# A decoder trunk on one core: the opening with x normalised ahead of its transposition, modulation tiles of two chunks, and every eighth tile summed on TensorE

## The reference

```python
h = rms_norm(x, g_pre) * (1.0 + scale) + shift
y = rms_norm(fn(h), g_post)
x = x + res_w * gate * y
```

## Time and profile before

| | us |
|---|---|
| median of three runs (lowest, highest) | 1993.89 (1992.87, 1994.47) |
| the profiled execution | 1992.25 |
| its span, first to last instruction | 1990.5 |
| PE busy in the span | 1892.8 (95%) |
| DVE busy | 1403.8 (71%) |
| ACT busy | 845.7 (42%) |

### The profile page before, as it was taken

One profiled execution on the slowest core, in us unless ns is written; L12 is line 12 of the kernel. 1 busy time (PEld: TensorE's weight loads), 2 busy tenths in 40 slices (PEclk: granted clock), 3 DMA queues, 4 the chain that ended last, 5 costly groups with the idle time before them and its releaser, 6 DMA issues.

```text
span 1990.5 us, 21378 instructions
## 1 busy us (share of the span) xinstructions
PE 1892.8 (95%) x8554; PEld 1538.5 (77%) x8554; DVE 1403.8 (71%) x1469; ACT 845.7 (42%) x1075; POOL 22.6 (1%) x29
## 2 busy tenths in 40 slices
PE   2679999999999999999999999999999999999997
PEld 2558878878878878777777787788888888888895
DVE  4997888878878878765766566666666665555556
ACT  2214434444443443474565533743444434443443
POOL 0000000000000000000000000000000000000000
PEclk7879999999999999999999999999999999999999
DMA  9898998998989988645333444566666665555551
GB/s 343 308 332 324 352 342 319 360 339 328 340 332 346 338 342 325 217 138 181 127 111 127 161 136 170 185 236 233 247 240 233 236 208 190 190 190 190 196 196 74
DMA packets 204131, 486.83 MB, mean 245 GB/s; under 512 B 8049, under 2 KB 21121, under 8 KB 188929
## 3 DMA queue, kind: packets, MB, share of 16 engines
q1 hardware_dynamic: 202816, 482.79, 68.0%
q10 hardware_dynamic: 992, 2.63, 0.4%
q0 software_dynamic: 224, 0.06, 0.0%
HBM read 483.31 MB, written 2.10 MB: 244 GB/s over the span
## 4 chain that ended last, share of the span: by engine, by line
PE 87%; DVE 5%; DMA 3%; issue 2%; ACT 1%; DVEq 0%; SPq 0%; POOLq 0%; POOL 0%; ACTq 0%
PE ps_g L1381 10%; PE ps_u L1381 10%; PE ps_u L1383 9%; PE ps_u L1382 9%; PE ps_g L1383 9%; PE ps_g L1382 9%; PE ps_t L1381 4%; PE ps_t L1382 4%; PE ps_t L1383 4%; PE ps_y L1383 4%; PE ps_y L1381 4%; PE ps_y L1382 4%; DVE arena L1144 2%; DMA ada_raw<-in_ada_w 2%; DVE w_lo L857 1%
## 5 line engine op out<-in xcount | busy, mean ns | idle before, releaser
L857 DVE TENSOR_TENSOR w_lo<-w_raw,w_hi 128x1024 fp32r<-128x1024 f32 (+1 forms) x632 | 752.9, 1200 | 481.0 <-ACT w_hi L509 479.8
L509 ACT ACTIVATE w_hi<-w_raw 128x1024 fp32r<-128x1024 f32 (+1 forms) x632 | 657.4, 1042 | 945.5 <-PE ps_u L1383 335.8
L1381 PE MATMUL ps_g<-w_hi,xT_hi 128*128 128x512 f32 (+1 forms) x880 | 346.9, 394 | 21.2 <-DVE w_lo L857 11.1
L1381 PE MATMUL ps_u<-w_hi,xT_hi 128*128 128x512 f32 (+2 forms) x880 | 348.1, 396 | 16.7 <-DVE w_lo L857 15.9
L1383 PE MATMUL ps_u<-w_hi,xT_lo 128*128 128x512 f32 (+2 forms) x880 | 342.3, 389 | 0.0
L1382 PE MATMUL ps_u<-w_lo,xT_hi 128*128 128x512 f32 (+2 forms) x880 | 341.8, 388 | 0.0
L1383 PE MATMUL ps_g<-w_hi,xT_lo 128*128 128x512 f32 (+1 forms) x880 | 340.8, 387 | 0.0
L1382 PE MATMUL ps_g<-w_lo,xT_hi 128*128 128x512 f32 (+1 forms) x880 | 340.5, 387 | 0.0
L881 DVE SCALAR_TENSOR_TENSOR arena<-ada_raw,cond,arena 128x2048 f32<-128x2048 f32 x108 | 253.5, 2347 | 24.4 <-DMA ada_raw<-in_ada_w 24.2
L1381 PEld LDWEIGHTS ps_g<-w_hi,xT_hi 128*128 128x128 f32 x880 | 165.9, 189 | 64.8 <-DVE w_lo L857 18.6
L1381 PEld LDWEIGHTS ps_u<-w_hi,xT_hi 128*128 128x128 f32 x880 | 167.0, 190 | 55.7 <-DVE w_lo L857 19.6
(11 more groups left out here) (242 smaller groups left out, 1542.3 us busy)
## 6 DMA issues: line engine op xcount, KB each, us to landing
w_raw<-in_ffn_w_in SPq DMA_DIRECT2D x160, 1024.0 KB, 5.1
ada_raw<-in_ada_w SPq DMA_DIRECT2D x128, 1024.0 KB, 7.3
w_raw<-in_ffn_w_out SPq DMA_DIRECT2D x80, 1024.0 KB, 5.1
w_raw<-in_mix_w_in SPq DMA_DIRECT2D x32, 1024.0 KB, 5.1
arena<-in_ada_w SPq DMA_DIRECT2D x16, 1024.0 KB, 10.2
w_raw<-in_mix_w_out SPq DMA_DIRECT2D x16, 1024.0 KB, 5.0
w_raw<-in_ffn_w_in SPq DMA_DIRECT2D x16, 768.0 KB, 4.5
w_raw<-in_ffn_w_out SPq DMA_DIRECT2D x8, 768.0 KB, 4.4
```

The costliest lines, as they stand in the source:

```text
L509: nc.scalar.activation(w_hi[:, u % 4, 0:n, 0:width], w_raw[:, s, 2 * hf:2 * hf + n, 0:width], ACT.Copy).then_inc(hi_done, 1)
L857: nc.vector.tensor_tensor(w_lo[:, u % 4, 0:n, 0:width], w_raw[:, s, 2 * hf:2 * hf + n, 0:width], w_hi[:, u % 4, 0:n, 0:width].bitcast(F32) ...
L1381: nc.tensor.matmul(o, a_hi[:, k, rows], w_hi[:, b, c, 0:width], start=start, stop=False)
```

## The change

- ACT's queue loads x in two halves instead of one piece; the four constant loads move to SP, after the tenth hidden block of the first SwiGLU, and DVE's wait for them to the token mixer.
- c has its own small load, transposition and semaphore, so that `cond` is made ahead of the other small columns.
- ACT squares x first. DVE makes the variance, POOL the power, ACT writes x times its row norm (128 x 2048, twice) into `yacc`, and only then PE transposes, into all eight PSUM banks. ACT copies the eight banks after the last transposition. The diagonal, its matmuls, `rbc` and `xt_scale` are gone.
- An `ada_w` tile now is two chunks of both vectors (two loads of 512 KB). DVE adds a chunk of both vectors in one operation of 128 x 1024, 14 operations a strip instead of 32, each waiting for the one before. The eighth tile of a strip isn't added on DVE: PE multiplies it by `cond` in the sums, 24 matmuls a strip instead of 16.
- A slot that the eighth tile used is loaded again only after the sums.
- After the columns, ACT makes scale and shift in one operation (two of 128 x 256, in place), waits for it, and copies 128 x 512 into `xT_hi`; DVE subtracts in one operation of 128 x 512.

```diff
-PRE_USES = 8
+PRE_USES = 16
-ADA_PRE = 32
+STRIP_TILES = 8
+STRIP_SUMMED = 7
+ADA_PRE = STRIPS * STRIP_SUMMED
@@ SP, a strip
-                for a in range(8):
-                    kg, m = divmod(a, 2)
-                    count = 8 * s + a
-                    need(sp, ada_done, count - 3)
-                    sp.dma_start(first_slots[a % 4]..., four chunks of one vector).then_inc(ada_landed[a % 4], 16)
+                for i in range(STRIP_TILES):
+                    if i % 4 == 3 and (s or i == 7):
+                        if i == 3:
+                            sp.wait_ge(cols_done, s)
+                        else:
+                            sp.wait_ge(ada_done, STRIP_SUMMED * s + 4)
+                    elif i >= 4:
+                        sp.wait_ge(ada_done, STRIP_SUMMED * s + i - 3)
+                    elif s:
+                        sp.wait_ge(ada_done, STRIP_SUMMED * (s - 1) + i + 5)
+                    for m in range(2):
+                        slot = first_slots[i % 4][:, m * 2 * NB:(m + 1) * 2 * NB].rearrange("p (k n) -> p k n", k=2)
+                        sp.dma_start(slot, ...[:, 2 * i:2 * i + 2, m * D + s * NB:m * D + (s + 1) * NB]).then_inc(ada_landed[i % 4], 16)
@@ ACT
+            def first_xt_hi(b):
+                act.wait_ge(modcol_done, b // 2 + 1)
+                for c in range(2):
+                    k = 2 * b + c
+                    ins = nc.scalar.activation(xT_raw[:, k, :], xT_raw[:, k, :], ACT.Identity, bias=modcol[:, 0, 1, k:k + 1],
+                                               scale=modcol[:, 0, 0, k:k + 1])
+                link(ins)
+                nc.scalar.activation(xT_hi[:, 2 * b:2 * b + 2, :], xT_raw[:, 2 * b:2 * b + 2, :], ACT.Copy).then_inc(xt_hi_done, 1)
...
+            first_x_squares()
+            act.wait_ge(rstd_ready, 1)
+            for t in range(TILES):
+                nc.scalar.activation(yacc[:, t, :], x_sb[:, t, :], ACT.Copy, scale=rstd[:, 2 + t:3 + t]).then_inc(xn_first, 1)
+            act.wait_ge(xt_done, 8)
             for b in range(8):
...
@@ DVE
+            def first_ada(s, i):
                 before = chain[0]
+                for k in range(2):
                     if k == 0:
+                        dve.wait_ge(ada_landed[i % 4], 32 * (2 * s + i // 4) + 32)
+                        need(dve, ada_done, STRIP_SUMMED * s + i if i else 0)
                     else:
+                        dve.wait_ge(dve_chain, before + 1)
+                    part = acc[:, 1:3, s * NB:(s + 1) * NB]
+                    raw = first_slots[i % 4].rearrange("p (m k n) -> p m k n", m=2, k=2)[:, :, k, :]
+                    weight = cond[:, 2 * i + k:2 * i + k + 1]
...
@@ PE, the sums of a strip
+                pe.wait_ge(ada_landed[3], 32 * (2 * s + 2))
+                pe.wait_ge(ada_done, STRIP_SUMMED * (s + 1))
                 for m in range(2):
+                    for c in range(4):
+                        for kk in range(2):
+                            nc.tensor.matmul(col, last[:, m, kk, c * P:(c + 1) * P], cond[:, 2 * STRIP_SUMMED + kk:2 * STRIP_SUMMED + kk + 1],
+                                             start=kk == 0, stop=False)
+                        ins = nc.tensor.matmul(col, acc[:, MODS_PRE[m][1], k * P:(k + 1) * P], ones[:, 0:1], start=False, stop=True)
```

More of the change, by code:

```diff
@@ L122, in build @@
         kvg = sb("kvg", [P, KV_RANK])
[L123 removed]
+        small_rows = sb("small_rows", [7 * KD, P])
         more_rows = sb("more_rows", [2 * KD, P])
@@ L1110, in xt_lo @@
-            def xt_lo(n, b):
-                def f():
-                    dve.wait_ge(xt_hi_done, 8 * n + b + 1)
-                    dve.wait_ge(xt_scaled, 8 * n + b + 1)
-                    for c in range(2):
-                        k = 2 * b + c
-                        last = nc.vector.scalar_tensor_tensor(xT_lo[:, k, :], junk[:, (k % 8) * SEQ:(k % 8 + 1) * SEQ], modcol[:, n, 1, k:k + 1],
-                                                              xT_hi[:, k, :].bitcast(F32), ALU.add, ALU.subtract)
-                    last.then_inc(xt_lo_done, 1)
-                return f
@@ L1121, in _ @@
-            dve.wait_ge(cond_ready, 1)
-            dve.wait_ge(const_landed, 16 * 4)
-            dve.wait_ge(ident_landed, 16)
-            nc.vector.tensor_scalar(negsink[:, :], sink[:, :], -1.0, None, ALU.mult)
-            def first_ada(s, kg):
+            def first_ada(s, i):
                 before = chain[0]
-                for i in range(8):
-                    k, m = divmod(i, 2)
-                    count = 8 * s + 2 * kg + m
-                    slot = (2 * kg + m) % 4
+                for k in range(2):
@@ L1133, in first_ada @@
                     if k == 0:
-                        dve.wait_ge(ada_landed[slot], 16 * (count // 4) + 16)
-                        if kg:
-                            dve.wait_ge(ada_done, count - 1)
-                    else:
-                        dve.wait_ge(dve_chain, before + i - 1)
-                    part = acc[:, MODS_PRE[m][1], s * NB:(s + 1) * NB]
-                    raw, weight = first_slots[slot][:, k * NB:(k + 1) * NB], cond[:, 4 * kg + k:4 * kg + k + 1]
-                    if kg == 0 and k == 0:
+                        dve.wait_ge(ada_landed[i % 4], 32 * (2 * s + i // 4) + 32)
@@ L1464, in gate_rows @@
                 ins.then_inc(gbc_done, 1)
-            def row_scale(n):
-                pe.wait_ge(diag_ready, n + 1)
-                for t in range(TILES):
-                    ins = nc.tensor.matmul(ps_y[:, 1, t * P:(t + 1) * P], ones[:, :], diag[:, t, :], start=True, stop=True)
-                ins.then_inc(rb_done, 1)
-                pe.wait_ge(rb_copied, n + 1)
             def warm(n, ps):
```

162 lines of the change are left out of this document (63 added, 99 removed).

## The result

| | before | after |
|---|---|---|
| median (lowest to highest), us | 1992.87 (1992.01 to 1994.47) | 2003.45 (1999.47 to 2006.92) |
| ratio, 95% interval | | 1.0056 [1.0038, 1.0073] |
| the profiled execution | 1992.25 | 1999.47 |
| end of the sums of strips 0, 1, 2, 3 | 46.8, 80.1, 112.7, 146.1 | 43.5, 76.5, 113.3, 149.2 |

The change is slower by 0.6%, where the prediction had it 0.5% faster (1983.1, range 1977 to 1989). The profiled execution after was the fastest of its five, 4 us under their median.

The account below looks back on a forecast made before the run. PE bounds the kernel, but DVE, with PE's sums in series, the opening. Strip 0 minus 7.3 us and the other strips minus 4.05 give -11.4; constants +0.6 make -10.8: 1981.4 profiled, 1983.1 median, range 1977 to 1989.

Parts of the forecast that it names:

- S3: End of the sums of strip 3, where the opening ends: 134.7 us forecast against 146.1, 11.4 earlier.
- the one on the sums: Sign on PE's sums at each strip's end: 24 sums take 1.5 times the 16 at the same clock.
- Start of strip 0: Strip 0's opening: DVE begins adding behind its variance at 15.65 us, adds end at 34.0, x copied by 32.8, hidden.
- The adds: DVE, strips 1 to 3: 20.7 us a strip become 17.5, minus 9.6 in all; dependent multiply-adds 1.31 us apart.
- After the columns: From columns to the next strip's first `w_lo`: DVE waits for ACT; plus 0.55 us in strip 0, together plus 1.35.
- DMA and the queues: Loads in the opening: 19 a strip instead of 11 and the lock on slot 3, costed at 0, slack 4 us.
- rivals 1 and 2: Opening's loads: half-size loads show fixed time, 1990.0 us, chance 0.12; the same with slot 3's lock, 1999.6, chance 0.04.
- Rival 3: PE's clock at the sums: all low 1987.0 us, all near full 1977.4; its two ends have chance 0.2.
- Rival 4: DVE's adds: two-chunk adds 0.22 us longer each, 3 us a strip, don't pay; 1995.4 us, chance 0.03.
- The constants: Four loads in the first SwiGLU, 0.46 MB ahead of an `ada_w` load: cost 0 to 1.2 us, taken as 0.6.
- R: The stretch after strip 3's sums: profiled execution less S3; a gain at S3 was to pass through it one for one.
- S0: End of the sums of strip 0: 39.4 us forecast against 46.74, 7.3 us earlier.

Follow-up runs that it names:

- experiment 3: Changed kernel without the eighth tile's products in the sums (its part left out of the result), loads and waits kept; median 1980.93 us, ratio 0.9937 to before.
- experiment 4: Changed kernel with all eight tiles added on DVE, 8 calls in a strip's sums, and constants loaded at the start; median 1987.71 us, ratio 0.9976 to before.
- experiment 1: Changed kernel with the four constant loads back on ACT's queue at the start, behind x; median 2000.82 us, ratio 1.0041 to before.
- experiment 5: Changed kernel with each of the 24 matmuls of the sums as its own group, nothing accumulating; 1999.28 us (one execution).
- experiments 8: Changed kernel with all eight tiles added on DVE and the constants loaded in the mixer; median 1987.94 us, ratio 0.9972 to before.
- experiment 10: Changed kernel, strip 0 adding eight tiles on DVE, strips 1 to 3 multiplying tile 3 early on PE, constants in the mixer; median 1983.27 us, ratio 0.9951 to before.
- run 13: Not named anywhere in the text given, which tells no change and no measured time for it.

## Why the prediction was wrong

**The step that failed is a term of the sum: "16 took 3.57 us at a granted clock of 0.50 and 1.95 at 0.89; 24 take 5.35 or 2.95".** The 16 was a count of records in the trace (x16), the 24 a count of calls in the diff. In the code before, line 1597 is called for m in 2 and k in 4: 8 times. The change makes that 24, three times as many and not half as many again. The sums were put at +6.0 us in all (1.8 in strip 0, 4.2 in the rest) and measured +19.6. The error of 13.6 us is nearly all of the 14.5 by which S3 missed (149.2 for 134.7). Of the signs named beforehand the one on the sums failed: at the same clock they took 10.37 us for 3.57, 2.9 times and not 1.5.

The trace of before had it in plain sight. Line 1463 is called four times, two into each buffer, and shows, on PE's timeline:

```profile
822.94 1.88 PE L1463 MATMUL ps_g<-arena,ones 128*128 128x512 f32 x4
824.65 1.88 PE L1463 MATMUL ps_u<-arena,ones 128*128 128x512 f32 x4
```

And the line 1471 of the earlier trace rows, from which I took "four 128 x 128 matmuls", is called twice. The transpositions are one record a call: 32 calls, x8 four times, the first of them

```profile
19.97 1.97 PE L1537 MATMUL ps_g<-ident,arena 128*128 128x128 f32 x8 [9.85 <-ACT arena L671]
```

So the 0.245 us that I gave each transposition was half a call of line 1471 and came out near (0.23) by luck. I had the loop bounds before me and wrote 16 a strip into the description of the kernel, and "24 instead of 16" into that of the change, where it is 24 instead of 8. The rows of line 1463 also give the price of f32: two calls over 512 columns take 824.65 - 822.94 = 1.71 us, 0.86 a call, where the f32r matmuls of the same width take 200 / 880 = 0.227, 3.8 times less. The Trainium skill says so, "FP8 and Floating Point Precision", section "TensorE Precision Notes": true FP32 makes four passes through the array. The trace agrees, as two records of twice the length. I didn't weigh that rule; by itself it would not have mended the sum, whose price was already that of f32 sums. What was missing is the two records a call.

The other steps, in order:

- *Start of strip 0*: DVE's variance starts at 14.54 and its first add at 14.62 (predicted 15.65), the adds end at 33.0 (34.0), x is copied at 30.34 (32.8, hidden as predicted). ACT's last copies, DVE's variance, and its adds:

```profile
29.20 1.14 ACT L674 ACTIVATE arena<-ps_y 128x512 f32<-128x512 f32 x2
...
14.54 0.17 DVE L1123 TENSOR_SCALAR ss<-ss 128x2 f32<-128x2 f32 x1 [14.54 <-ACT arena L586]
...
15.40 3.99 DVE L1095 SCALAR_TENSOR_TENSOR arena<-ada_raw,cond,arena 128x1024 f32<-128x1024 f32 x3
...
24.92 5.31 DVE L1095 SCALAR_TENSOR_TENSOR arena<-ada_raw,cond,arena 128x1024 f32<-128x1024 f32 x4
```

- *The adds*: 1.284 us each (1.279 predicted), but 1.35 apart, not 1.31: in the fence, x4 last 5.31 us, so three gaps of (5.31 - 1.28) / 3 = 1.34, and from 15.40 to 24.92 seven pass in 9.52 us, 1.36 each. The hand-over between two dependent adds is 0.07 us here, not the 0.03 that I took from two column operations. Over 13 adds that is 0.5 to 0.6 us a strip, some 1.7 in strips 1 to 3. Strips 1 to 3 without their sums shrank by 6.4 us in all (91.1 to 84.7), for 8.25 predicted: this is nearly all of the difference. The rule in the Trainium skill, "VectorE: DVE Perf Modes", section "The DRAIN you can't avoid", that a semaphore between such operations costs nothing would have had them 1.20 apart by the prediction's estimate, still further off.
- *After the columns*: DVE waits for ACT (7.3 us in six waits), and in strip 0 the first `w_lo` starts at 48.40, 4.5 us after the columns' end (4.25 predicted); in strip 1 the next strip's first `w_lo` starts at 82.31, 5.4 us after (5.2 predicted).
- *DMA and the queues* (rivals 1 and 2): neither. No addition of strips 1 to 3 waited for a load, and 387 GB/s are reached with halves of 512 KB queued (first row of the windows on the sums; from 38 us on, with the 1 MB weight loads before them landed, it is 388). The advice of 1 MiB or more in "DMA: Bandwidth & Descriptors" of the Trainium skill, section "Bandwidth", does not bind here, where loads queue behind each other. The lock on slot 3 is in experiment 3 too, where no addition of strips 1 to 3 waits for a load.
- *Rival 3*, the clock: the sums ran at 0.50, 1.00, 0.64 and 0.71. Its price was mis-sized with the sums: between the two levels lie 5.0 us a strip (10.37 and 5.41), not 2.4.
- *Rival 4*: the two-chunk adds pay; experiment 4, with eight of them, is 5 us faster than before.
- *The constants*: 0.6 us predicted ("0 to 1.2"), R rose by 3.8 to 4.5. I bounded it by their bytes at 387 GB/s. The load behind them took 2.9 us longer to land than before, which is about their bytes (1.2) and the gap in the transfers (1.6). R in the four kernels with this place is 1850.2 to 1853.2, in the four with the start 1846.1 to 1847.1. The four with the mixer's place have 1848.2 to 1849.6, so some 2 us of the rise are there too, without that gap in this stretch: the bytes and the gap can account for the rest only.

In sum, for the profiled executions: 13.6 (sums) + 0.9 (adds slower, start earlier) + 3.5 (constants, 4.1 for 0.6) = 18.0, which is 1999.47 less the 1981.4 predicted. The medians differ by 2.3 us more; the five executions after spread over 7.5 us.

The mechanism "a gain at S3 passes to the end one for one" held in the main: S3 ranges from 129.0 to 170.0 us over the kernels, and R from 1846.1 to 1853.2, in three groups by the place of the constants. It is closest with them at the start (R within 1 us over 31 us of S3); with the late place R grew by 3.0 us where S3 fell by 20.3. The forecast failed on the size of one term. With the right one the same working gives S0 = 34.05 + 10.7 = 44.75, and for the other three strips 99.4 - 8.25 plus 7.8 (all sums at full clock, 16.05 for 8.24) to 23.9 (all at the low one): S3 at 143.7 to 159.8, from 2.4 us earlier to 13.7 later than before. No rival had it; all kept the 24 to 16.

**What stays open.** With the constants in the mixer R is 1848.2 to 1849.6, some 2 us over the start's place, though nothing is moved into the stretch that differs (the last 110 us before the gates of the first SwiGLU, where DVE waits 9.2 to 12.5 us for `ada_w` loads; in three kernels with the start's place it waits 8.3 to 9.8). A shift of the loads against the additions is my guess; it wasn't tested. Nor was it tested why the kernel after spreads more than the one before; that the sums' clock differs between executions would do it, but each kernel has one profile, so what is seen is only that it differs between kernels (strip 1 in experiment 1, strip 2 in experiment 5).

## What to carry to other kernels

Count instructions in the code and records in the trace, and divide the one by the other before scaling anything; an x16 in a profile is not sixteen calls. Work that moves to an engine which is idle "anyway" is free only if it doesn't stand in the series that everything waits for: here 16 calls a strip cost 5.1 us ((149.23 - 128.98) / 4) between the last addition and the columns, where the same tile costs 2.4 us on DVE ((138.53 - 128.98) / 4, experiments 8 and 3), and nothing that shows in strips 1 and 2 of experiment 10, where they run 13 to 14 us ahead of the sums. A small load put into a running stream can cost more than its bytes: look at what the load behind it makes its reader wait.

## What the runs showed of the hardware

- An f32 matmul is two records with two weight loads, at 1, 128 and 512 columns alike, while an f32 transposition is one: one column costs 0.43 to 0.44 us a call at a granted clock of 0.50 (10.40 / 24) and 0.225 at full clock (5.41 / 24), with a weight load in each record. A chunk of both vectors needs eight such calls, 1.8 to 3.5 us, and one operation of 1.28 us on DVE.
- The granted clock at the start of short work after a wait can't be read off the instructions: the same sums of strip 1 ran at 1.00 in one kernel and at 0.64, mostly low, in another whose only difference was the place of four loads, in one profile of each.
- Four constant loads of 0.46 MB together, two of them broadcast to 128 partitions, put into the stream of large loads, were followed by 1.2 to 2 us in which the DMA engines all but stood, in the four kernels that have them there. In the gap of the kernel after 101 of 118 packets are the 64-byte ones of the 8 KB `sink`, and where they pass at the start DMA moves 154 GB/s for 394 without them; moving that load alone wasn't tried.
